# Third tile of a depthwise convolution moved from VectorE to GpSimd

## The reference, cut to what matters

```python
def conv_module(zc, w_dw, b_dw, ln_g, ln_b, w_pw, b_pw):
    a, gt = jnp.split(zc, 2, axis=-1)
    v = a * jax.nn.sigmoid(gt)
    v = lax.conv_general_dilated(v, w_dw[:, None, :], window_strides=(1,),
                                 padding=[(15, 15)],          # CONV_K = 31 taps
                                 feature_group_count=384) + b_dw   # CONV_CH = 384
    v = layer_norm_2(v, ln_g, ln_b)
    return jax.nn.silu(v) @ w_pw + b_pw
```

## Time and profile before

| | us |
|---|---|
| median of 3 runs | 3133.84 (3133.8 to 3136.14) |
| the profiled execution | 3133.42 |
| its span | 3131.7 |
| busy PE, DVE, ACT, POOL | 2974.7, 2060.2, 1368.2, 139.6 |
| 180 taps at L1530 | 62.9 (512 columns, 90) and 37.5 (256 columns, 90 of them) |

### The profile page before, as it was taken

One profiled execution on the slowest core, in us unless ns is written; L12 is line 12 of the kernel. 1 busy time (PEld: TensorE's weight loads), 2 busy tenths in 40 slices (PEclk: granted clock), 3 DMA queues, 4 the chain that ended last, 5 costly groups with the idle time before them and its releaser, 6 DMA issues.

```text
span 3131.7 us, 52116 instructions
## 1 busy us (share of the span) xinstructions
PE 2974.7 (95%) x19700; PEld 2674.8 (85%) x19700; DVE 2060.2 (66%) x3303; ACT 1368.2 (44%) x2222; POOL 139.6 (4%) x205
## 2 busy tenths in 40 slices
PE   8998998997999999999889999999999999889898
PEld 8888998887999988897568888888998889769898
DVE  4657785557677777768843365767767667775655
ACT  4554444454445432354542254222542225654444
POOL 0000000000000000010000020100201002000000
PEclk9999999998999999999999999999999999999999
DMA  6435664435565565551103354544545445216454
GB/s 229 138 105 169 228 234 163 137 105 164 195 214 179 193 214 191 174 182 62 57 25 96 98 169 154 195 154 174 184 147 201 149 147 174 88 49 189 155 186 143
DMA packets 147696, 486.16 MB, mean 155 GB/s; under 512 B 16320, under 2 KB 25792, under 8 KB 147392
## 3 DMA queue, kind: packets, MB, share of 16 engines
q1 hardware_dynamic: 126640, 407.22, 38.9%
q0 software_dynamic: 20880, 76.56, 7.1%
HBM read 482.66 MB, written 1.05 MB: 154 GB/s over the span
## 4 chain that ended last, share of the span: by engine, by line
PE 80%; DVE 11%; ACT 5%; issue 3%; DMA 1%; DVEq 0%; POOLq 0%; ACTq 0%; SPq 0%
PE bank L1783 22%; PE bank L1785 22%; PE bank L1784 22%; DVE wlo L1012 4%; ACT whi L542 2%; PE bank L1727 2%; PE bank L1728 2%; PE bank L1729 2%; DVE acc L1530 1%; PE bank L2000 1%; PE bank L1858 1%; PE aux L1984 1%; PE aux L2077 1%; DVE small L1545 1%; PE bank L1803 0%
## 5 line engine op out<-in xcount | busy, mean ns | idle before, releaser
L1783 PE MATMUL bank<-uhi,whi 128*128 128x256 f32 (+1 forms) x4000 | 1250.0, 313 | 15.9 <-DVE wlo L1012 9.3
L1012 DVE TENSOR_TENSOR wlo<-raw,whi 128x1024 fp32r<-128x1024 f32 (+4 forms) x850 | 949.0, 1118 | 479.1 <-ACT whi L542 477.0
L1784 PE MATMUL bank<-ulo,whi 128*128 128x256 f32 (+1 forms) x4000 | 1237.8, 309 | 0.0
L1785 PE MATMUL bank<-uhi,wlo 128*128 128x256 f32 (+1 forms) x4000 | 1237.7, 309 | 0.0
L542 ACT CAST whi<-raw 128x1024 fp32r<-128x1024 f32 (+4 forms) x850 | 806.0, 961 | 270.0 <-PE bank L1785 170.7
L1783 PEld LDWEIGHTS bank<-uhi,whi 128*128 128x128 f32 x4000 | 757.4, 189 | 78.6 <-issue 22.0
L1784 PEld LDWEIGHTS bank<-ulo,whi 128*128 128x128 f32 x4000 | 757.7, 189 | 44.8 <-issue 0.2
L1785 PEld LDWEIGHTS bank<-uhi,wlo 128*128 128x128 f32 x4000 | 757.4, 189 | 44.6
L1783 PE MATMUL bank<-yhi,whi 128*128 128x256 f32 (+1 forms) x1432 | 443.6, 310 | 21.2 <-DVE wlo L1012 14.4
L1784 PE MATMUL bank<-ylo,whi 128*128 128x256 f32 (+1 forms) x1448 | 444.9, 307 | 0.0
L1785 PE MATMUL bank<-yhi,wlo 128*128 128x256 f32 (+1 forms) x1432 | 439.4, 307 | 0.0
(11 more groups left out here) (266 smaller groups left out, 2962.9 us busy)
## 6 DMA issues: line engine op xcount, KB each, us to landing
raw<-in_w_stream SPq DMA_DIRECT2D x674, 512.0 KB, 3.5
big<-in_w_ada POOLq DMA_DIRECT2D x64, 512.0 KB, 3.8
vt<-in_w_ada POOLq DMA_DIRECT2D x51, 512.0 KB, 3.8
raw<-in_w_stream SPq DMA_DIRECT2D x80, 256.0 KB, 2.7
raw<-in_w_stream SPq DMA_DIRECT2D x48, 384.0 KB, 3.1
bbb<-in_w_ada POOLq DMA_DIRECT2D x29, 512.0 KB, 3.9
raw<-in_w_stream SPq DMA_DIRECT2D x32, 192.0 KB, 2.4
raw<-in_w_stream SPq DMA_DIRECT2D x16, 128.0 KB, 2.0
```

The source lines that it names most:

```text
L1012: ve.tensor_tensor(wlo[:, u % SLOTS, 0:n], raw[:, u % SLOTS, 0:n], whi[:, u % SLOTS, 0:n].bitcast(F32), ALU.subtract).then_inc(s_low, 1)
L1783: te.matmul(out_, whi[:, u % SLOTS, w], hi(k)[:, c0:c1], start=k == 0, stop=False)
L1784: te.matmul(out_, whi[:, u % SLOTS, w], lo(k)[:, c0:c1], start=False, stop=False)
L1785: ins = te.matmul(out_, wlo[:, u % SLOTS, w], hi(k)[:, c0:c1], start=False, stop=k == plan.kt[u] - 1)
```

## The change

GpSimd does all 31 taps of the third tile, in both layers. A tap, which is one instruction on DVE, is two there: a `tensor_scalar` into a scratch buffer and a `tensor_tensor` that adds it to `acc`; the first tap is one `tensor_scalar`. That is 61 instructions for a layer, each waiting for the one before (`s_tap`). The scratch is `vpad[:, 0]`, the first tile's input; so GpSimd waits for the third tile's input (`s_vpad`) and for DVE's last tap of the first tile (`s_conv`). DVE runs the first tile's 31 taps one behind the other, then the second's, 62 for a layer, and each tap waits for the one right before it. The numbers that are issued at each place change: in layer 0 6 in each of the last four mix steps as before, then 2 in place of 3 in each of 8 Fourier steps, 2 in each of 8 kv steps as before, and the last 6 in attention. In layer 1 6 in place of 4 in each of four mix steps, 5 in place of 6 in each of 4 Fourier steps, 2 in each kv step, and the last 2 in attention, where there were 37.

```diff
             seams = {"fup102": (0, 1), "fup200": (0, 1), "fup202": (0, 1), "fup112": (1, 0)}
-            added, squared = Tally(pool, s_add), Tally(pool, s_hsq)
+            convolutions = {"fup102": 0, "fup112": 1}
+            added, squared, tapped = Tally(pool, s_add), Tally(pool, s_hsq), Tally(pool, s_tap)
+
+            def convolve(l):
+
+                c0 = S if l == L - 1 else 0
+                w, b = p2("w_dw", l, TAPS * CT), p2("b_dw", l, CT)
+                m = CT - 1
+                pool.wait_ge(s_vpad, l + 1)
+                pool.wait_ge(s_conv, (CT - 1) * l + 1)
+                product, a = vpad[:, 0, c0 // S:2, 0:S], acc[:, m, c0:T2].rearrange("p (s t) -> p s t", t=S)
+                for k in range(TAPS):
+                    v, wk = vpad[:, m, c0 // S:2, k:k + S], w[:, k * CT + m:k * CT + m + 1]
+                    if k:
+                        tapped.wait()
+                    if k == 0:
+                        tapped.add(nc.gpsimd.tensor_scalar(a, v, wk, b[:, m:m + 1], ALU.mult, ALU.add))
+                        continue
+                    tapped.add(nc.gpsimd.tensor_scalar(product, v, wk, None, ALU.mult))
+                    tapped.wait()
+                    ins = nc.gpsimd.tensor_tensor(a, a, product, ALU.add)
+                    if k < TAPS - 1:
+                        tapped.add(ins)
+                    else:
+                        ins.then_inc(s_pconv, 1)
...
                 for s in seams.get(name, ()):
                     add_squares(s)
+                if name in convolutions:
+                    convolve(convolutions[name])
...
                     self.l, self.c0, self.at, self.last = l, c0, 0, [0] * CT
+                    self.n = TAPS * (CT - 1)
...
-                    for _ in range(min(n, TAPS * CT - self.at)):
-                        k, m = self.at // CT, self.at % CT
+                    for _ in range(min(n, self.n - self.at)):
+                        k, m = self.at % TAPS, self.at // TAPS
...
                     if n < LN_AT[l]:
-                        conv.taps(-(-(TAPS * CT - conv.at) // (LN_AT[l] - n)))
+                        conv.taps(-(-(conv.n - conv.at) // (LN_AT[l] - n)))
...
-                        step.add(ve.tensor_tensor(
+                        ins = ve.tensor_tensor(
                             vpad[:, m, s0:2, PAD:PAD + S],
                             big2[:, 4 + m, c0:T2].rearrange("p (s t) -> p s t", t=S),
-                            acc[:, m, c0:T2].rearrange("p (s t) -> p s t", t=S), ALU.mult))
-                        conv.last[m] = step.n
+                            acc[:, m, c0:T2].rearrange("p (s t) -> p s t", t=S), ALU.mult)
+                        if m == CT - 1:
+                            ins.then_inc(s_vpad, 1)
+                        else:
+                            step.add(ins)
+                            conv.last[m] = step.n
...
                     if j >= 12:
-                        conv.taps(4 if last else 6)
+                        conv.taps(6)
...
-                    conv.taps(6 if last else 3)
+                    conv.taps(5 if last else 2)
...
                         for m in range(CT):
-                            pe.wait_ge(s_conv, CT * l + m + 1)
+                            pe.wait_ge(*((s_conv, (CT - 1) * l + m + 1) if m < CT - 1 else (s_pconv, l + 1)))
                             ins = te.matmul(banks[3][:, c0:T2], ones, acc[:, m, c0:T2], start=m == 0, stop=m == CT - 1)
```

More of the change, by code:

```diff
@@ L400, in program @@
         s_conv = sem("convolved")
+        s_pconv = sem("pool_convolved")
+        s_tap = sem("pool_tap_done")
+        s_vpad = sem("pool_conv_input_ready")
         s_centred = sem("conv_centred")
```

## The result

The kernel before took 3133.84 us (median of 5 runs, 3130.79 to 3138.03), the changed one 3163.91 us (median of 5, 3153.89 to 3168.97): a ratio of 1.0084, with an interval of 1.0063 to 1.0106. The ratio is not the quotient of the two medians, which is 1.0096 and lies inside the interval. It is slower, by 30 us by the medians and 26 by the ratio. The forecast was 3187, 53 us slower: the sign and the place were right, the size was about twice what came. The profiled execution of the changed kernel took 3156.8 us (span 3155.1), 23.4 more than the profiled one of before; the changed kernel's runs lie 15 us apart, and this one is in their lower half.

What follows compares the result with a forecast made beforehand. PE, 95% busy, was taken to bound the kernel, with DVE counting only where PE waits for it. Layer 0's +33 and layer 1's +21 us on 3133.4 gave 3187 us, range 3131 to 3215 (likeliest case 3154 to 3207).

Steps and rivals of the forecast that it cites:

- What bounds it, and the mechanism: PE bounds the kernel; DVE and POOL instructions with two SBUF inputs take turns, mostly in kv and q; chance 0.68.
- The order of the taps: Mix and Fourier steps: each chained tap 0.10 us longer; layer 1's Fourier starts 2.8 us later, ends 4.8 later.
- The relief in attention: Attention: fewer DVE taps shorten PE's waits by 3.4 us in layer 0 (3 counted) and 3.5 in layer 1.
- The price of a meeting: DVE beside POOL: 512-column add costs 1.0 us, product 0.5; mean 0.75 in layer 0, 0.38 in layer 1.
- the number of meetings: Kv and q: 24 and 20 DVE instructions a layer each meet POOL; +30.8 us layer 0, +14.6 layer 1.
- Nothing to feel: Whole kernel: POOL uses DVE's gaps, so only tap order and attention relief count; about 0, 3133 us; chance 0.14.
- faster: Whole kernel: no lock felt, chained taps free, attention relief stays; -6.5 us, 3127 us; chance 0.08.
- The tile comes late: Layer 1's norm: above 1.44 us an instruction PE waits for POOL; at 1.7 us +16, 3203 us; chance 0.10.

Runs made afterwards that it cites:

- order_alone: The changed kernel with POOL doing only the third tile's first tap, the other 30 left out in each layer: 3133.58 us, 1.0009 of the kernel before.
- relief_alone: As order_alone, but DVE alternates between its two tiles and POOL's one tap no longer waits for the first tile: 3129.53 us, 0.9988 of the kernel before.
- changed_again: The changed kernel itself, unaltered, timed and profiled again beside the other runs: 3159.63 us, 1.0087 of the kernel before.
- adds_alone: The changed kernel with POOL's 30 products a layer left out, its first tap and 30 adds kept: 3156.62 us, 1.0082 of the kernel before.
- late_start: The changed kernel with DVE alternating between its two tiles, nothing left out, so POOL starts only in attention: 3215.56 us, 1.0260 of the kernel before.

## Where the prediction was right, and the step that failed

**What bounds it, and the mechanism: right.** The cost sits where the prediction put it, in kv and q, and there in DVE's instructions with two SBUF inputs. POOL and DVE take turns; POOL gets in between DVE instructions that have no gap (the timelines above). The Trainium skill (SBUF — State Buffer, "SBUF: two separate sides") holds that whichever of the two starts first keeps the shared ports for its whole instruction. For the adds the trace agrees (1.0 of 1.18 us felt). For the one-operation product it does not: 0.3 to 0.43 us felt of 1.57.

**The order of the taps: right.** DVE's timeline of layer 0's mix steps has six chained taps in 4.68 us, 4.06 before; start to start that is (4.68 - 0.75) / 5 = 0.79 us against 0.66, +0.13 a tap where 0.10 was taken from the rotary rows.

```profile
1450.35 4.68 DVE L1560 SCALAR_TENSOR_TENSOR acc<-vpad,par,acc 128x512 f32<-128x512 f32 x6
```

Layer 1's Fourier stage starts 3.0 us later in place of 2.8. With POOL at rest (order_alone) it ends 5.0 later, where 4.8 was forecast. At the level of the kernel the chain is worth at most about the 0.2% between order_alone and relief_alone.

**The relief in attention: right in layer 1, wrong in layer 0.** Layer 1's attention has 50.4 - 44.1 = 6.3 us of idle PE before and 2.7 after: 3.6, where 3.5 was taken; another 2.1 are shorter busy time, at a mean clock of 0.96 in place of 0.95. In layer 0 the idle time is 14.6 us before and 14.9 after, 12.9 in changed_again: between none and 1.7 of the 3.4 came. The 5.1 that the stage gained in the first profile is busy time at a higher clock, so that it beats the forecast of 3 is luck; in changed_again it gained 1.8. With POOL at rest (order_alone) idle time in layer 0's attention is 87.2 - 74.1 = 13.1 us, so fewer taps gave back 1.5 there. The prediction took it that what DVE's waits lose is gained: they fell by 2.7 (from 12.2 less 2.9 of filling to 9.3 less 2.8), but PE's wait for ACT's probabilities grew from 2.9 to 4.4.

**The price of a meeting: right.** An add of 512 columns was taken at 1.0 us: the `low` lost 1.0, and adds_alone 0.91 an instruction. A product was taken at 0.5: the pair of taps lost 0.43 to one. That half was a choice between two bounds, because a product reads one tensor in place of two, and that it came out near is in part luck: no run shows that reason, and the product is longer than the add, 1.57 against 1.18. POOL's groups by line and shape in the changed kernel (busy, mean ns, idle before):

```profile
L504 POOL TENSOR_SCALAR vpad<-vpad,par 128x512 f32<-128x512 f32 x30 | 53.4, 1780 | 2.9
L506 POOL TENSOR_TENSOR acc<-acc,vpad 128x512 f32<-128x512 f32 x30 | 40.0, 1332 | 2.5
```

**The step that failed: the number of meetings.** The terms are "kv: 8 steps with a `low` and two taps each, 24 x 0.75 = 18.0" and the same in "q: 20 x 0.75", which let each of 44 DVE instructions a layer meet an instruction of POOL at the mean price. In kv and q POOL issued 31 instructions in layer 0 and 34 in layer 1. The timelines show one pair of POOL's instructions for three of DVE's: POOL needs 1.62 + 1.42 us and its two hand-overs, 3.22 in all, and DVE does its three in that time. So a kv step lost 1.0 + 0.43, not 3 x 0.75 = 2.25: 3.22 - 1.78 = 1.44 us by the rows. Over eight steps that is 11.5 in place of 18.0 (from PE's first kv matmul to DVE's first rotary instruction it grew by 29.67 - 18.72 = 10.95). q and the rest gave 5.0 in place of 12, and in layer 1 kv and q gave 5.0 in place of 14.6. POOL's other instructions ran in attention, where 12 of layer 0's 30 adds fall and where DVE has room (55.8 us busy of 88.5): POOL lasted almost 100 us (1472.21 to 1571.94), 80 had been expected. adds_alone is the control: with an add always ready, the count of the prediction came true (4.52 a step, 1.78 + 3 x 0.91), and with it kv and q took 14.2 us more than in order_alone, from 22 adds.

The count is not the whole of it. By DVE's busy time in kv and q, against order_alone, POOL cost DVE 17.5 us in layer 0 where the prediction had 44 x 0.75 = 33, and 6.6 in layer 1 where it had 44 x 0.38 = 16.7. Fewer instructions at the predicted prices make 9.8 and 3.8 of the gap; the other 5.7 and 6.3 are instructions of POOL that cost DVE less than the mean price (0.57 each in layer 0, 0.19 in layer 1, although a meeting in layer 1's kv cost the predicted 0.45 and 0.23). That these fell where DVE stood idle or ran an instruction that doesn't clash is likely, but no run shows it. More idle time of DVE hiding the cost isn't the reason: the stages grew by 14.3 and 5.0 over order_alone, so it hid 3.2 and 1.6 us, where 3 and 3 had been taken off.

**The rivals.** "Nothing to feel" and "faster" fell: order_alone, which has only their terms, is at 1.0009, the change at 1.0084. The sum of "nothing to feel", about 0, was right for the terms that it has. "The tile comes late" fell for this kernel (L2050 waits for nothing, in layer 1 POOL ends at 2789.3 and the norm's first matmul is at 2796.9), but its margin of 7 us in layer 1 is thin, and late_start shows its price.

**The size.** The sum of the stages was predicted as 54 and is 20.9; the medians are 30 apart. The stages of changed_again sum to 25.7, nearly all of the 24.4 us between its profiled execution (3157.83) and that of before. The 2.5 us between table and profiled executions of the first profile, and the 7 between those and the medians, aren't placed.

## What to carry to other kernels

Work moved to GpSimd beside a busy VectorE isn't free for VectorE: price each of its instructions by what DVE loses to it, by kind, not by duration (here an add of 512 columns 1.0 us, a product 0.3 to 0.43, a tap on DVE itself 0.66), and multiply by how many GpSimd can issue in the stretch, which goes by its own time for a pair, not by how many DVE instructions lie there. That is an upper bound: over whole stages the price of one was lower. In layer 0's kv a tap on POOL cost DVE 1.4 us in place of the 0.66 that it saved.
Before you build such a move, leave the work out altogether and time that: relief_alone would have shown a ceiling of 0.12%.

## What the runs showed of the hardware

- GpSimd's `tensor_scalar` with one operation takes 1.57 us for 512 columns, with two operations 0.70 (0.90 for the first tap, L502). The Trainium skill (GPSIMD Engine Reference, "Engine selection") calls one-input work roughly line rate. For the form with one operation the trace doesn't agree: a `tensor_tensor` add with two inputs took 1.18, less than this product with one.
- The longer product hurts DVE less than the shorter add: 0.43 against 1.0 us.
- A DVE instruction with one SBUF input (128x256 scaling) went from 0.35 to 1.08 us beside POOL; the prediction had priced only instructions with two.
- Two dependent DVE instructions in a row start 0.10 us (rotary) to 0.13 us (taps) later than independent ones.
- The granted clock moves busy time between stages and between executions: over the seven stages PE was busy 214.7 us before, and 214.7 and 221.6 in two profiles of the changed kernel. Stages are better compared by PE's idle time than by their length.
